# A prefetch hint for the closing branch of the loops of TensorE, VectorE and ScalarE

## The reference

```python
z = jnp.einsum('btd,df->btf', u, w_qkv).reshape(b, t, N_DGROUPS, 3, N_HEADS, HEAD_DIM)
q = rms_norm(z[:, :, :, 0], q_gain[:, None, :])
k = rms_norm(z[:, :, :, 1], k_gain[:, None, :])
...
for g, (win, dil) in enumerate(zip(WINDOWS, DILATIONS)):
    o, l = dilated_band(q[:, :, g], k[:, :, g], v[:, :, g], win, dil, tab)
o = merge_groups(outs, lses)          # softmax over the three groups
...
a = jnp.einsum('td,edf->tef', ub, wg)  # every expert e; gates are zero but for two
c = jnp.einsum('td,edf->tef', ub, wu)
hh = jax.nn.silu(a) * c * gb[:, :, None]
return jnp.einsum('tef,efd->td', hh, wd)
```

## Time and profile before

| | us |
|---|---|
| median of 3 executions | 1272.0 |
| lowest, highest | 1271.73, 1274.61 |
| the profiled execution: its own time | 1273.8 |
| its span, first to last instruction | 1272.0 |
| mean granted clock of TensorE in it | 0.915 of full |
| PE busy | 1142.9 (90%) |
| DVE, ACT, POOL busy | 428.3, 224.4, 225.1 |
| DMA moved | 462.64 MB |

### The profile page before, as it was taken

How to read it: one execution, slowest core, us unless ns; L and a number is a source line. 1 busy time by engine, 2 the same in 40 slices (tenths; PEclk the granted TensorE clock), 3 DMA queues, 4 the chain that set the end, 5 groups by cost and what they waited for, 6 DMA issues and landing times.

```text
span 1272.0 us, 16186 instructions
## 1 busy us (share of the span) xinstructions
PE 1142.9 (90%) x5441; PEld 736.3 (58%) x5442; DVE 428.3 (34%) x843; ACT 224.4 (18%) x508; POOL 225.1 (18%) x484
## 2 busy tenths in 40 slices
PE   5999799999949899974999999999474999999998
PEld 2887688778822688863455455554353455545554
DVE  3356456755820466123111011112733111101113
ACT  1122122122110144111111111111001111111110
POOL 1014212411410122002022222210002022222210
PEclk9999899999957699975899999999665899999999
DMA  9999999999789988899999999999999699999996
GB/s 372 332 380 379 397 387 359 342 398 386 273 291 357 395 263 292 333 364 322 329 431 429 428 398 405 417 392 389 377 335 332 263 390 392 388 390 392 399 423 229
DMA packets 62931, 462.64 MB, mean 364 GB/s; under 512 B 12112, under 2 KB 20192, under 8 KB 47888
## 3 DMA queue, kind: packets, MB, share of 16 engines
q1 hardware_dynamic: 49136, 440.29, 89.5%
q0 software_dynamic: 5536, 18.88, 4.0%
q10 hardware_dynamic: 8232, 3.13, 1.0%
HBM read 455.19 MB, written 183.41 MB: 502 GB/s over the span
## 4 chain that ended last, share of the span: by engine, by line
PE 59%; DVE 7%; issue 3%; DMA 3%; ACT 1%; POOL 1%; ACTq 1%; POOLq 0%; DVEq 0%; SPq 0%
PE bank L1228 17%; PE bank L1214 11%; PE bank L1254 8%; PE bank L1203 5%; PE bank L1165 2%; PE bank L1097 2%; DMA region_a<-in_w_up_dram 2%; PE bank L1124 1%; PE bank L1132 1%; PE bank L1144 1%; PE bank L1175 1%; PE bank L285 1%; PE bank L1260 1%; PE bank L1104 1%; PE bank L1121 1%
## 5 line engine op out<-in xcount | busy, mean ns | idle before, releaser
L1053 PE MATMUL bank<-uT,ring_lo 128*128 128x264 f32 x1152 | 273.9, 392 | 8.5 <-DVE uT L298 6.0
L1053 PEld LDWEIGHTS bank<-uT,ring_lo 128*128 128x128 f32 x1152 | 218.0, 194 | 48.8 <-issue 9.7
L1214 PE MATMUL bank<-scratch 128*128 128x128 f32 (+1 forms) x768 | 149.3, 328 | 18.0 <-POOL scratch L568 18.0
L1214 PEld LDWEIGHTS bank<-scratch 128*128 128x128 f32 (+1 forms) x768 | 113.9, 204 | 50.6 <-POOL scratch L568 18.2
L783 DVE RECIPROCAL scratch<-scratch 128x264 f32<-128x264 f32 x48 | 86.5, 1802 | 112.0 <-ACT scratch L630 112.0
L1228 PE MATMUL bank<-ring_lo,scratch 128*64 128x512 f32 x512 | 117.5, 613 | 0.0
L1254 PE MATMUL bank<-ring_lo,scratch 128*64 128x512 f32 x512 | 113.4, 595 | 0.8 <-issue 0.8
L1228 PE MATMUL bank<-region_a,scratch 128*64 128x512 f32 x512 | 112.6, 592 | 0.9 <-DMA region_a<-in_w_up_dram 0.9
L959 DVE TENSOR_TENSOR scratch<-bank,scratch 128x512 f32<-128x512 f32 x16 | 11.1, 692 | 291.6 <-PE bank L1228 291.6
L553 POOL TENSOR_TENSOR small<-epsc 128x1 f32<-128x1 f32 x83 | 16.0, 195 | 387.4 <-PE bank L1260 334.8
L1228 PEld LDWEIGHTS bank<-region_a,scratch 128*64 128x64 f32 x512 | 37.0, 137 | 73.9 <-issue 73.9
(11 more groups left out here) (220 smaller groups left out, 1206.4 us busy)
## 6 DMA issues: line engine op xcount, KB each, us to landing
out_dram<-in_cache_kv_w_dram SPq DMA_DIRECT2D x128, 1023.5 KB, 18.0
ring_lo<-in_w_gate_dram SPq DMA_DIRECT2D x32, 2048.0 KB, 12.0
region_a<-in_w_up_dram SPq DMA_DIRECT2D x32, 2048.0 KB, 15.2
ring_lo<-in_w_down_dram SPq DMA_DIRECT2D x32, 2048.0 KB, 16.1
ring_lo<-in_w_qkv_dram SPq DMA_DIRECT2D x18, 2048.0 KB, 17.0
out_dram<-in_cache_kv_w_dram SPq DMA_DIRECT2D x32, 1022.0 KB, 33.2
ring_lo<-in_cache_kv_w_dram POOLq DMA_DIRECT2D x24, 512.0 KB, 10.4
ring_lo<-in_cache_kv_w_dram SPq DMA_DIRECT2D x6, 2048.0 KB, 13.8
```

Source lines behind the costliest of these rows:

```text
L1053: last = mm(z_bank[s % 4][:, 0:T], w[:, k, at:at + P], uT[:, k, :], start=(k == 0), stop=(k == KT - 1))
L1214: last = mm(bank[m // 4][:, m % 4 * P:(m % 4 + 1) * P], u_tok[0:sizes[b], b, m * P:(m + 1) * P], pick[0:sizes[b], b, :], start=(b == 0), s ...
```

## The change

```diff
             eng.wait_ge(rounds_ready, layer + 1)
-            with eng.Fori(0, NP) as p:
+            with nc.Fori(0, NP, engines=[eng.engine], hint_back_edge=True) as p:
                 first, end = (eng.value_load(rounds_i[0:1, ds(p + (layer * (NP + 1) + n), 1)], min_val=n, max_val=MAX_ROUNDS)
                               for n in range(2))
...
-                with eng.Fori(first, end) as q:
+                with nc.Fori(first, end, engines=[eng.engine], hint_back_edge=True) as q:
                     one_round(q, p)
...
-            with ac.Fori(0, G) as g:
+            with nc.Fori(0, G, engines=[ac.engine], hint_back_edge=True) as g:
...
-            with ac.Fori(1, H // 4) as i:
+            with nc.Fori(1, H // 4, engines=[ac.engine], hint_back_edge=True) as i:
...
-            with dve.Fori(0, G) as g:
+            with nc.Fori(0, G, engines=[dve.engine], hint_back_edge=True) as g:
...
-            with dve.Fori(1, H // 4) as i:
+            with nc.Fori(1, H // 4, engines=[dve.engine], hint_back_edge=True) as i:
...
-            with pe.Fori(0, G) as g:
+            with nc.Fori(0, G, engines=[pe.engine], hint_back_edge=True) as g:
...
-            with pe.Fori(1, H // 4) as i:
+            with nc.Fori(1, H // 4, engines=[pe.engine], hint_back_edge=True) as i:
```

## The result

The changed kernel takes 1280.85 us, the median of 5 runs (1280.15 to 1282.65); the kernel before took 1272.1 us beside it (5 runs, 1271.73 to 1274.61). The ratio is 1.0064, with a 95% interval of 1.005 to 1.0079 (written [1.005, 1.0079] from here on): **slower**, a small loss of 0.6% that is clear of noise. The medians lie 8.75 us apart, and the forecast was 1272.4 with a range that ended at 1276.5. The two profiled executions, 1273.8 and 1280.85, are 7.05 us apart; these are the microseconds that the traces can place.

What follows compares the result with a forecast made beforehand. PE was taken to bound the kernel, busy 1142.9 of 1272.0 us. Nothing removed and seven exposed hints adding 0.39 us gave 1272.0 + 0.4 = 1272.4 us, range 1270.5 to 1276.5.

Steps and rivals of the forecast that it cites:

- Queues of kind "instruction", nothing returns: Projection and experts' loops: bodies are brought once and kept, queue 8 absent in the second pass; no back edge stalls a microsecond.
- What is removed: 0: All hinted loops: no wait, transfer or instruction goes; counted 0, with -0.8 us from PE's two projection returns as bound.
- what is added: 55 ns for each hint: Heads of the eight loops: one sequencer instruction per pass, seven of them exposed, 0.39 us in all.
- Heads: cost 0: Heads' loop: hints hidden, DVE by 1.3 us of cover, ACT's and PE's by queued work; cost 0.
- The slow rival: Seven exposed loop heads: each hint refetches the head's block or displaces one needed next; 1282 to 1309 us, chance 0.09.
- its weaker form: A hint cost staying on one engine or coming only with wrong hints: up to 1279 us, chance 0.03 above the 0.3% bound.
- The term of a fetch: Price of one instruction fetch at a loop head: 1.4 us from queue 8's share, 3.3 us from a small waited-for transfer.
- The second cause named for a miss: Code standing one instruction further on meets a block's end where an engine has no cover; no size given.
- The test "queue 8 has 15 pieces as before": Sign in the profile after: an unchanged piece count was expected; many more would show hints fetching what is there.
- After an idle stretch the clock falls: Projection, PE: after 1.19 us idle the granted clock is 0.50 from 144 to 150 us; slightly more idle changes nothing.

Runs made afterwards that it cites:

- experiment 1: Changed kernel without DVE's hint at the projection loop (L773), other hints kept: 1278.11 us against 1277.84 for the kernel before, ratio 1.0004.
- experiment 3: Kernel before with DVE's hint at the projection loop (L773) as its only hint: 1284.24 us, ratio 1.0052 to the kernel before.
- experiment 4: Changed kernel with DVE's hint at L773 replaced by a one-column memset that keeps later code in place: 1278.08 us, ratio 1.0004 to the kernel before.
- experiment 2: Changed kernel without DVE's hint at the heads' loop (L864), other hints kept: 1284.65 us, ratio 1.006 to the kernel before.
- experiment 5: Changed kernel, all hints kept, with DVE's projection loop head (L773) placed at slot 80: 1282.36 us against 1277.65 for the kernel before, ratio 1.0051.
- experiment 6: Kernel before with 384 filler memsets in DVE's projection body, making about 557 instructions, no hints: ratio 1.0042 to the kernel before.
- experiment 10: Kernel before, no hints, with five unused reciprocals on DVE once ahead of the fourth head: 1281.49 us, ratio 1.0031 to the kernel before.
- experiment 7: Kernel before with 384 filler memsets in DVE's projection body and, as only hint, DVE's at L773: ratio 1.0098 to the kernel before.
- experiment 8: Kernel before with DVE's hint at L773 as only hint and that loop's head at slot 80: ratio 0.9999 to the kernel before.
- experiment 9: Kernel before with DVE's projection loop head (L773) at slot 80 and no hint: ratio 0.9995 to the kernel before.

## Why the prediction was wrong

- *Queues of kind "instruction", nothing returns*: right. The projection's body is held, there is no stall at a back edge, and the hint had nothing to win. PE's branch still takes 0.226 us at the median.
- *What is removed: 0*, *what is added: 55 ns for each hint*: right. The hints take 31 to 60 ns, and no stretch of projection or experts shows more than that. Nor do they stop at a wrong guess: the 16 inner ones, whose branch is never taken, last 31 ns on POOL.
- **The step that failed is "Heads: cost 0".** I costed a hint where it stands, by the cover that its engine has there. DVE's hint of the projection is hidden in the projection, as said; it is paid 115 instructions behind its loop, in the heads, where 1.3 us of cover meet 4.89 us. In the place of the 0 stand 3.7 us of PE's idle time (3.39 and 0.27) and 3.1 us of low clock.
- *The slow rival* had the right thought in half a sentence, "or the block takes the place of one needed next", and the wrong price and place. It was costed at seven loop heads with 1.4 to 3.3 us each and came to 1282 to 1309. The runs show one place that costs, 4.9 to 5.5 us of DVE's. The time measured, 1280.85, lies between this rival's range and its weaker form's (up to 1279), so neither had the size; the side had been given 0.12. Most of the effect lies in one of eight statements (experiments 1 and 3).
- *The term of a fetch was too small.* It was estimated at 1.4 us from queue 8's share, or 3.3 us from a small transfer; the stalls for one measured 4.9 to 5.5 us. The share of a queue tells how long packets occupy the engines, not how long a sequencer waits from asking to going on.
- *The second cause named for a miss*, code that stands one instruction further on: wrong (experiment 4), though it pointed at the right symptom, a block's end without cover.
- *The test "queue 8 has 15 pieces as before"* held and said nothing. PE's displaced block is still fetched once, only later, and the count is the same; experiments 1, 2 and 5 even have 14 there. Only the windows show it.
- *After an idle stretch the clock falls*: the prediction used it for the projection alone, where the clock was low already. In the heads it nearly doubles the loss.

What stays open: L285's 16 matmuls take 5.49 us after and 3.83 before (this and the line of before, from the timelines of PE):

```profile
556.40 5.49 PE L285 MATMUL bank<-scratch,ones 128*128 128x264 f32 x16 [2.52 <-ACT scratch L290]
```

```profile
550.31 3.83 PE L285 MATMUL bank<-scratch,ones 128*128 128x264 f32 x16 [2.52 <-ACT scratch L290]
```

The granted clock falls earlier here, which costs 1.66 us; this stands in experiments 3, 6 and 10 as well (5.25 to 5.51 us) and in none of the others, so it comes with and without a hint and with and without the stall, and no run tells why. It accounts for the last microsecond: 6.09 + 1.66 = 7.75 us, of which 7.05 are left at the end. Nor is it settled why the medians lie 8.75 us apart where the traces lie 7.05 apart; experiments 2 and 3 gave 6.8 and 6.4 us for the same stall. Shown is that with the hint a block isn't fetched ahead and that DVE stands where it needs it; why the hint does this is not, and neither the engine nor the target of a transfer is in the trace. The best version found is the kernel before.

## What to carry to other kernels

Before hinting a loop, look for a stall between its branch and its next instruction, and for pieces of kind "instruction" during its second pass; where there are none, the hint has nothing to win in what these runs show. Cost an instruction that steers the fetch not only where it stands but also where the engine leaves the code that it holds, behind the loop, and ask what cover the engine has there. Where PE is the bound, a stall's price can be more than its length: in two of these kernels idle time of 1.9 and 3.4 us cost about 3 us again by the lower clock. It need not be so: L285 stands behind 2.52 us of idle time in both kernels, and took 3.83 us in one and 5.49 in the other.

## What the hardware showed that was not expected

- A branch prefetch hint takes 31 to 60 ns (kernel after), but the next block of the program is not fetched ahead. DVE then stood for 4.9 us (after), 5.4 us (experiment 2) and 5.5 us (experiments 3 and 7) at one instruction.
- A fetch that is waited for is long: 4.9 to 5.5 us for a piece of 8,192 bytes on queue 14. The transfer is the small part of it: in the kernel after it takes 0.3 us (0.5% of 16 engines for 4 us, at 462.25), some 3 us after DVE's last work, and DVE goes on 1.6 us after its start.
- For a body that does not fit, the hint shortened DVE's returns from 6.5 and 8.8 us to 4.9 and 5.0 us.
- A jump to a placed loop head costs 2.7 to 3.7 us at the entry (experiments 5, 8 and 9), of which PE felt nothing measurable in experiments 8 and 9.
